# One core, fp32 in split parts: the feed-forward products in another shape in each of four layers

## The reference

```python
# first block
gu = rms_norm(x, norm_ffn[l]) @ w_gate_up[l]                       # 1024 -> 2 * 2816
x = x + (jax.nn.silu(gu[..., :D_FF]) * gu[..., D_FF:]) @ w_down[l]  # 2816 -> 1024

# layers 0 to 3
def conv_ffn(h, w_up, dw_w, dw_b, w_down):
    u = dwconv(h @ w_up, dw_w, dw_b)
    val, gate = jnp.split(u, 2, axis=-1)
    return (jax.nn.gelu(gate) * val) @ w_down
```

## Time and profile before

| | |
|---|---|
| median of 3 runs | 3131.26 us (3128.67 to 3132.65) |
| span of the profiled execution | 3131.9 us, 0.6 us above the median |
| instructions | 35714, 14221 of them matmuls |
| busy share of the span | PE 99%, PEld 79%, POOL 48%, DVE 45%, ACT 41% |
| granted clock of TensorE | 0.998 of full speed over the span |

### The profile page before, as it was taken

One profiled execution on the slowest core, in us unless ns is written; L12 is line 12 of the kernel. 1 busy time (PEld: TensorE's weight loads), 2 busy tenths in 40 slices (PEclk: granted clock), 3 DMA queues, 4 the chain that ended last, 5 costly groups with the idle time before them and its releaser, 6 DMA issues.

```text
span 3131.9 us, 35714 instructions
## 1 busy us (share of the span) xinstructions
PE 3095.4 (99%) x14221; PEld 2463.3 (79%) x14221; DVE 1418.0 (45%) x2646; ACT 1273.2 (41%) x1972; POOL 1498.4 (48%) x734
## 2 busy tenths in 40 slices
PE   9999999999999999999999999999999999999999
PEld 6668888875788887778888888888888887588887
DVE  5564111188643345445343544423534358753433
ACT  5463222256433335553333333323433337543332
POOL 2225555566454453334554534444454557545554
PEclk9999999999999999999999999999999999999999
DMA  5212333344232333222323322222333335323232
GB/s 192 73 48 88 101 94 94 101 116 128 82 106 90 97 105 101 95 81 89 101 94 98 109 75 80 81 81 75 94 101 94 94 101 136 102 94 101 88 101 88
DMA packets 90038, 303.11 MB, mean 97 GB/s; under 512 B 10128, under 2 KB 10384, under 8 KB 89744
## 3 DMA queue, kind: packets, MB, share of 16 engines
q1 hardware_dynamic: 89152, 299.73, 31.1%
q10 hardware_dynamic: 720, 1.10, 0.1%
HBM read 281.42 MB, written 2.10 MB: 91 GB/s over the span
## 4 chain that ended last, share of the span: by engine, by line
PE 87%; DVE 8%; ACT 2%; DMA 1%; issue 1%; SPq 0%; POOL 0%; ACTq 0%; DVEq 0%
PE PS L1483 26%; PE PS L1485 25%; PE PS L1484 25%; DMA PT<-PD 1%; DVE XH L2096 1%; PE PS L1669 1%; DVE XL L2098 1%; PE PS L1506 1%; PE PS L1497 1%; PE PS L1495 1%; PE PS L1496 1%; DVE PS L2392 1%; PE PS L1510 1%; DVE X L2124 1%; PE PS L1562 1%
## 5 line engine op out<-in xcount | busy, mean ns | idle before, releaser
L2555 POOL TENSOR_TENSOR WL<-RAW,WH 128x1024 fp32r<-128x1024 f32 x503 | 1211.3, 2410 | 1250.3 <-ACT WH L1780 1250.0
L1483 PE MATMUL PS<-XH,WH 128*128 128x512 f32 x2640 | 1057.9, 401 | 3.1 <-DVE XL L2112 2.2
L1485 PE MATMUL PS<-XH,WL 128*128 128x512 f32 x2640 | 1030.7, 390 | 0.0
L1484 PE MATMUL PS<-XL,WH 128*128 128x512 f32 x2640 | 1029.9, 390 | 0.0
L1780 ACT ACTIVATE WH<-RAW 128x1024 fp32r<-128x1024 f32 x503 | 528.1, 1051 | 449.5 <-PE PS L1485 437.4
L1483 PEld LDWEIGHTS PS<-XH,WH 128*128 128x128 f32 x2640 | 496.2, 188 | 141.8 <-issue 34.0
L1484 PEld LDWEIGHTS PS<-XL,WH 128*128 128x128 f32 x2640 | 496.9, 188 | 106.7 <-issue 8.6
L1485 PEld LDWEIGHTS PS<-XH,WL 128*128 128x128 f32 x2640 | 496.2, 188 | 105.3
L1483 PE MATMUL PS<-HH,WH 128*128 128x512 f32 x1264 | 494.7, 391 | 10.1 <-POOL WL L2555 5.7
L1485 PE MATMUL PS<-HH,WL 128*128 128x512 f32 x1264 | 492.8, 390 | 0.0
L1484 PE MATMUL PS<-HL,WH 128*128 128x512 f32 x1264 | 492.7, 390 | 0.0
(11 more groups left out here) (269 smaller groups left out, 2383.0 us busy)
## 6 DMA issues: line engine op xcount, KB each, us to landing
RAW<-wst SPq DMA_DIRECT2D x503, 512.0 KB, 3.5
PT<-PD SPq DMA_DIRECT2D x32, 260.0 KB, 5.0
BI<-natb SPq DMA_DIRECT2D x16, 384.0 KB, 4.4
PT<-PD SPq DMA_DIRECT2D x20, 258.0 KB, 4.8
X<-xin SPq DMA_DIRECT2D x16, 256.0 KB, 4.7
PT<-PD SPq DMA_DIRECT2D x8, 262.0 KB, 4.9
X<-cmpw SPq DMA_DIRECT2D x1, 2048.0 KB, 13.0
out<-X SPq DMA_DIRECT2D x8, 256.0 KB, 2.0
```

What stands on the lines that cost most here:

```text
L1483: e.matmul(o, wh, h, start=first, stop=False)
L1484: e.matmul(o, wh, l, start=False, stop=False)
L1485: t = e.matmul(o, wl, h, start=False, stop=last)
L2555: e.tensor_tensor(WL[:, b % NSPLIT, :], RAW[:, b % NRAW, :], WH[:, b % NSPLIT, :].bitcast(f32), SUB).then_inc(*did(lo_made, ("lo", b)))
```

## The change

Four of the five feed-forward parts get a shape of their own for their matmuls; the fifth (layer 3) and all other products stay as they are.

- First block, "strided": two neighbouring weight tiles are interleaved column by column in the weight stream (on the host, before the launch), so that a tile's 128 columns lie at every second element. The two loads of WH and the one of WL read with a step of 2 elements.
- Layer 0, "halves": each matmul of 512 moving columns becomes two of 256, on the two halves of the same bank, each with its own load of the same weight tile.
- Layer 1, "turned": the three parts come in the order WH high, WL high, WH low.
- Layer 2, "backwards": the moving operand and the bank are walked from the last column to the first (step of -1 element), in all three matmuls.

```diff
--- before.py
+++ after.py
@@ -88,6 +88,14 @@
     return (0, wide(name), True), (wide(name), mc, False)
 
 
+SHAPES = {"ffn": "strided", "ffn2_0": "halves", "ffn2_1": "turned", "ffn2_2": "backwards"}
+
+
+def shape_of(name):
+    return SHAPES.get(name[:name.rindex("_")], "plain")
+
+
+TILE_SHAPES = [shape_of(name) for name, k, m in linears() for _ in range(k * m)]
 N_TILES = sum(k * m for _, k, m in linears())
 N_BLOCKS = (N_TILES + 7) // 8
 
@@ -330,7 +338,8 @@
                 ends = k == kc - 1
                 group = ("group", state["tile"])
                 events = ((("used", b),) if closes else ()) + ((group,) if ends else ())
-                step("mac", bank.ap, (*(bank.free if k == 0 else ()), made), k == 0, ends, b, j, h, l, events)
+                step("mac", bank.ap, (*(bank.free if k == 0 else ()), made), k == 0, ends, b, j, h, l, events,
+                     TILE_SHAPES[state["tile"] - 1])
                 return group
 
             def first_wide(mv, evac, mid, late):
@@ -1475,11 +1484,31 @@
         def tensor(e):
             w = Waits(e)
 
-            def mac(i, o, after, first, last, b, j, h, l, events):
+            def mac(i, o, after, first, last, b, j, h, l, events, shape):
                 wh, wl = (x[:, b % NSPLIT, 128 * j:128 * j + 128] for x in (WH, WL))
                 for event in after:
                     w.wait_ge(*at(event))
                 w.wait_ge(*at("lo_first" if b == 0 and j < 4 else ("lo", b)))
+                if shape == "strided":
+                    c = 256 * (j // 2) + j % 2
+                    wh, wl = (x[:, b % NSPLIT, c:c + 255:2] for x in (WH, WL))
+                elif shape == "backwards":
+                    o, h, l = (bass.AP(x.tensor, x.offset + T - 1, [x.ap[0], [-1, T]]) for x in (o, h, l))
+                if shape == "halves":
+                    for y, x, starts, ends in ((wh, h, first, False), (wh, l, False, False), (wl, h, False, last)):
+                        for c in (slice(0, 256), slice(256, 512)):
+                            t = e.matmul(o[:, c], y, x[:, c], start=starts and c.start == 0, stop=ends,
+                                         skip_group_check=True)
+                    if events:
+                        t.then_inc(*did(pe_made, *events))
+                    return
+                if shape == "turned":
+                    e.matmul(o, wh, h, start=first, stop=False)
+                    e.matmul(o, wl, h, start=False, stop=False)
+                    t = e.matmul(o, wh, l, start=False, stop=last)
+                    if events:
+                        t.then_inc(*did(pe_made, *events))
+                    return
                 e.matmul(o, wh, h, start=first, stop=False)
                 e.matmul(o, wh, l, start=False, stop=False)
                 t = e.matmul(o, wl, h, start=False, stop=last)
@@ -2715,6 +2744,9 @@
         w = w.reshape(kc, 128, mc, 128)
         for a, b, by_chunk in spans(name, mc):
             part = w[:, :, a:b].transpose((0, 2, 1, 3) if by_chunk else (2, 0, 1, 3)).reshape(-1, 128, 128)
+            if shape_of(name) == "strided":
+                part = part.reshape(-1, 2, 128, 128).transpose(0, 2, 3, 1).reshape(-1, 128, 2, 128).transpose(0, 2, 1, 3)
+                part = part.reshape(-1, 128, 128)
             flat[at:at + len(part)] = part
             at += len(part)
     wst = np.ascontiguousarray(flat.reshape(N_BLOCKS, 8, 128, 128).transpose(0, 2, 1, 3)).reshape(
```

## The result

The changed kernel takes 3171.82 us (median of 3 runs, 3171.40 to 3172.11) against 3131.26: a ratio of 1.0129, 95% interval 1.0111 to 1.0147, slower by 40.6 us. The profiled execution spans 3170.0 us, 38.1 more than before.

What follows compares the result with a forecast made beforehand. PE bounds the kernel, through the distance from one matmul to the next. Terms 0 + 21.2 + 0 + 0 took the profiled span from 3131.9 to 3153.1; the median stood 0.6 lower, so 3152 us, range 3117 to 3215.

Steps and rivals of the forecast that it cites:

- the likeliest case: Whole kernel: only the halves cost, +21.2 us, the other three shapes 0; 3152 us, own range 3147 to 3158, chance 55%.
- What bounds the kernel: Feed-forward stretches: PE alone sets their end, by the distance between matmuls, 226.7 ns; PE busy 99% of the span.
- a fixed price of 13.4 ns per matmul: Layer 0: each matmul pays 13.4 ns over its columns whatever their number, so a pair of halves takes 240.1 ns, +21.2 us.
- the 430 ns that bounded the first block and the walk from above: Distance of f32 matmuls of 512 columns, taken as PE's slowest; upper ends +337 us for first block, +322 us for layer 2.
- it stays hidden as long as it takes less than twice its 110 ns: First block: a stepped load has room for one factor of two beside the matmul, so it costs 0.
- Rival 2: First block: each stepped load takes cycles from the matmul beside it, 13.4 ns each, +21 us more, 3173 us; chance 8%.
- neighbours in memory are still neighbours in time: Layer 2: walking by -1 still reads and writes neighbours one after another, so the backward walk costs 0.
- rival 3: Layer 2: the backward walk falls out of pairs and takes two cycles a column, +322 us, 3474 us; chance 17%.
- rival 5: Any unseen walk: one costs up to 40 ns a product, 63 us, time up to 3215 us; chance 7%.

Runs made afterwards that it cites:

- e1: Changed kernel with layer 0's halves put back to 512 columns, the other shapes kept: 3151.16 us, ratio 1.0061 to the kernel before.
- e3: Kernel before, walks apart and combined: moving backwards costs 10.5 us, bank backwards 359.9 us, both plus stepped loads 370.4; halves with stepped loads 120.1 ns, walked backwards 118.5.
- e6: Kernel before, operands as f32: pass of 512 columns 428.9 ns, of 256 215.8; backwards 1360.0 us, stepped loads 1360.1; 256 at moving step 2 226.7 ns.
- e8: Kernel before, moving operand read by every 2nd, 4th, 8th, 16th or 32nd line, then the others: 233.4, 226.7, 246.7, 278.1, 267.9 ns a matmul.
- e2: Kernel before, only weight loads changed, to steps 4, 8, 3, 2 (WL alone) and 0: means 235.1, 244.6, 234.5, 231.2, 231.8 ns a matmul.
- e4: Kernel before, other moving sizes and steps: 256 at step 2 226.7 ns, 128s 111.7, 384 and 128 286.9, 128s at step 4 118.7, 320 and 192 258.9.
- e7: Kernel before, moving operand reordered: pairs exchanged or lines reversed 359.9 us, second half first costs nothing, blocks of 16 backwards 370.5 us, 510 columns from column 1 233.4 ns.
- e5: Kernel before, loads of 64 columns 229.4 ns a matmul, 32 columns 235.5, 64 with halves 116.8; matmuls of 128 columns with loads of step 4 233.4, step 2 117.8.

## Why the prediction was right and where it was not

Direction and range held: 3171.8 lies in 3117 to 3215, slower was given 90%. The forecast of 3152 was short by 20 us, and the time lies outside the likeliest case's own range of 3147 to 3158. Two of the four shapes failed the prediction's own signs, by which the stretches of the first block and of layer 2 had to stay at 360 us and over 365 meant a mistake: both are 370.4 or 370.5. The parts' measured 42.1 us against 21.2 are the 20 us.

- What bounds the kernel: right. In all nine profiles of changed kernels the feed-forward stretches are PE's and its loads' alone, and each change of a matmul's distance came out in the time whole, as e1 shows.
- Halves: +21.2 forecast, +21.1 measured, 120.0 ns where 120.1 was expected. The size was right, but the reason behind it (a fixed price of 13.4 ns per matmul) was not: the price is 118.5 less 106.7 = 11.8 ns for halves walked backwards (e3), 2.5 for f32 passes (e6), and up to 65 by the order of lines (e8). For the plain forward walk it happened to be the same for 256 and 512 columns. The 2.5 ns of the Trainium skill (TensorE: Matmul & The Clock Gate, "Back-to-back issue gap") are found here in the f32 rows, not for fp32r.
- The rows for f32 were read as whole matmuls. They are passes, two for a matmul (e6), so the 430 ns that bounded the first block and the walk from above are not the slowest way in which PE takes columns: a whole f32 matmul of 512 takes 858. No result came near that bound.
- Turned order: 0 forecast, 359.9 us before and now.
- Interleaved weights: 0 forecast, +10.4 measured. The step that failed is "it stays hidden as long as it takes less than twice its 110 ns". The load did stay hidden, at 193 ns for 188. What I left out of the sum is that a hidden load can slow the matmul that hides it. Rival 2 named this, and expected 13.4 ns a matmul from twice the lines; 6.7 were measured, and e2 shows that the lines a load touches do not set it. That rival 2's 3173 is near the result is chance: it was reached by 10.4 + 10.6, not by its own 21.
- Backward walk: 0 forecast, +10.6 measured. The step that failed is "neighbours in memory are still neighbours in time". So far the step held that the walk did not cost two cycles a column, as rival 3 had it and as a step of 2 does (e4). But it costs 6.7 ns, all of it in reading (e3), by the order in which it comes to the lines (e7, e8): neighbours in a line are not all that counts. My rival 5 covered a price of up to 40 ns without a mechanism.

What the experiments show of the cause of both is which side of the matmul it lies on: the load's step for the first block (e1, e2), the order of lines in which the moving operand is read for layer 2 (e3, e7, e8). Behind that stands a reading of mine: PE's reads of the moving operand and those of the load beside it get in each other's way where the moving side needs every access. These speak for it: the price all but goes where the reader has time to spare (f32 passes, with either walk), returns when that is used up (f32 at step 2), changes with the order of lines on one side (e8) and with the step on the other (steps 2, 3 and 0 in e2), and is not additive (e3). That the two meet at all, in banks of the memory or elsewhere, was not shown. No run has matmuls without a load beside them, so a moving reader that pays for its order by itself is a rival left standing, and that stepped loads and the backward walk cost 233.4 ns each and together is also what two separate limits give, of which the longer counts; against the second speaks that a load of step 2 by itself takes 117.8 ns (e5). It stays open why step 2 and the backward walk cost exactly 16 cycles each, why the distance grew with smaller loads, and whether an order exists with a mean under 13.3 ns over the columns.

## What to carry to other kernels

Where matmuls stand back to back, measure the distance of starts per shape and take it apart into columns and the rest; that a load is hidden says nothing of what it costs the matmul that hides it. With fp32r at one column a cycle the moving operand should be read in neighbouring floats, line after line upwards, and from column 0 rather than 1: a step of 2 doubled the time of a column, and of the other orders of lines one cost nothing in the mean and the rest 3 to 23% of a matmul of 512. Splitting a matmul of 512 columns in two costs 13 ns; writing the bank backwards, exchanging the parts of a product and reading pairs or lines reversed cost nothing.

## What the runs showed that I had not expected

- A moving step of 2 floats takes two cycles a column in fp32r (226.7 ns for 256 columns), while loads keep nearly their length at step 2 (193 ns for 188).
- Where all matmuls have 128 columns, the loads limit them to one in 111.7 ns at step 1, 117.8 at step 2 and 233.4 at step 4.
- In pairs of 384 and 128 columns the distances are 228 and 58 ns; only their sum, 286.9, fits a price for each matmul.
- In the stretch with loads of step 4 the granted clock fell from 1.00 to the lower level, 0.50, after 5.8 us and stayed there for the other 1474 us, although PE shows no idle time there or in the 250 us ahead of it; matmuls of 128 columns with a load before each, one in 233 ns, are all that it did.
- An f32 matmul is recorded as two passes of 2 cycles a column.
- With loads of 32 or 64 columns beside 512 moving columns, and matmuls that write as many rows, the distance was longer (235.5 and 229.4 ns against 226.7).
